# Twenty instead of sixteen tokens of the second tile gathered in the expert layer, 172 instead of 176 dense columns

## What is computed

```python
def one_block(xb):                                   # rows of h, width 2048
    q = (xb @ w_pq).reshape(TOKEN_BLOCK, PEER_HEADS, PEER_DKEY)      # 8 heads, key 256
    s1 = jnp.einsum('thd,kd->thk', q[..., :half], sub_k1)            # 128 keys
    s2 = jnp.einsum('thd,kd->thk', q[..., half:], sub_k2)            # 128 keys
    v1, i1 = lax.top_k(s1, PEER_TOPK)                                # 16
    v2, i2 = lax.top_k(s2, PEER_TOPK)
    best, pos = lax.top_k(cand, PEER_TOPK)                           # of 16 x 16 sums
    eidx = jnp.take_along_axis(cidx, pos, axis=-1)                   # i1 * 128 + i2
    gate = jax.nn.softmax(best.astype(jnp.float32), axis=-1)
    u = expert_u[eidx]                                               # 16384 experts, 2048 wide
    act = jax.nn.gelu(jnp.einsum('td,thkd->thk', xb, u), approximate=False)
    vv = expert_v[eidx]
    return jnp.einsum('thk,thkd->td', gate * act, vv)
```

## Time and profile before

| | |
|---|---|
| median of 3 runs | 2197.24 us |
| the profiled execution | 2204.14 us, span 2202.3 us |
| PE busy | 2130.4 us, 97% |
| DVE busy | 1266.8 us, 58% |
| ACT / POOL busy | 299.2 us / 372.1 us |
| DMA | 853.72 MB, mean 388 GB/s; 838.39 MB read from HBM |
| queues | SP's 47.7%, POOL's 39.5%, ACT's 8.1% of 16 engines' span |

### The profile page before, as it was taken

One profiled execution on the slowest core, in us unless ns is written; L12 is line 12 of the kernel. 1 busy time (PEld: TensorE's weight loads), 2 busy tenths in 40 slices (PEclk: granted clock), 3 DMA queues, 4 the chain that ended last, 5 costly groups with the idle time before them and its releaser, 6 DMA issues.

```text
span 2202.3 us, 36988 instructions
## 1 busy us (share of the span) xinstructions
PE 2130.4 (97%) x14900; PEld 2037.0 (92%) x14900; DVE 1266.8 (58%) x2329; ACT 299.2 (14%) x951; POOL 372.1 (17%) x414
## 2 busy tenths in 40 slices
PE   8999998898899999999999999999999999999997
PEld 6799996686699989999999999999999999999996
DVE  4454447534575378688885467778544444444445
ACT  3000007412310121111111013222000000000002
POOL 0000001123111012222221122222111111111210
PEclk9999999999999999999999999999999999999998
DMA  8999997699698979999999999999999999999996
GB/s 333 405 410 416 394 367 295 243 404 409 245 355 353 366 301 364 387 417 419 422 420 422 420 417 413 413 394 420 420 422 422 422 422 422 421 422 420 420 422 247
DMA packets 126497, 853.72 MB, mean 388 GB/s; under 512 B 14560, under 2 KB 24928, under 8 KB 39488
## 3 DMA queue, kind: packets, MB, share of 16 engines
q1 hardware_dynamic: 58416, 424.43, 47.7%
q0 software_dynamic: 54128, 354.58, 39.5%
q10 hardware_dynamic: 13856, 73.41, 8.1%
HBM read 838.39 MB, written 81.05 MB: 417 GB/s over the span
## 4 chain that ended last, share of the span: by engine, by line
DMA 57%; PE 20%; DVE 13%; issue 5%; ACT 3%; POOL 1%; SPq 0%; DVEq 0%; POOLq 0%; ACTq 0%
DMA BIG<-expert_v,VB 28%; DMA BIG<-expert_u,VB 20%; PE low L1573 11%; PE big L1573 9%; DMA WR<-wall 6%; DVE BIG L1388 4%; DVE XT L1401 3%; DMA BIG<-kaT 2%; DMA BIG<-va 1%; DVE BIG L1328 1%; ACT BIG L710 1%; DVE BIG L1325 1%; DVE BIG L1332 0%; ACT BIG L722 0%; POOL BIG L601 0%
## 5 line engine op out<-in xcount | busy, mean ns | idle before, releaser
L1573 PE MATMUL low<-HT,WR 128*128 128x176 f32 (+3 forms) x6040 | 896.3, 310 | 10.6 <-DVE BIG L1023 7.1
L1573 PEld LDWEIGHTS low<-HT,WR 128*128 128x128 f32 x6040 | 883.7, 191 | 14.0 <-issue 9.3
L1401 DVE SCALAR_TENSOR_TENSOR XT<-BIG,VB,XT 128x2048 f32<-128x2048 f32 x128 | 301.0, 2351 | 341.5 <-DMA BIG<-expert_v,VB 341.4
L1573 PE MATMUL big<-BIG,WR 128*128 (+4 forms) x2952 | 451.0, 308 | 2.5 <-DMA WR<-expert_v 1.8
L1573 PEld LDWEIGHTS big<-BIG,WR 128*128 128x128 f32 x2952 | 430.5, 192 | 4.7 <-issue 3.1
L1388 DVE SCALAR_TENSOR_TENSOR BIG<-BIG 128x2048 f32<-128x2048 f32 x144 | 329.8, 2291 | 179.6 <-DMA BIG<-expert_u,VB 178.1
L1573 PE MATMUL low<-BIG,WR 128*128 (+3 forms) x2552 | 415.8, 318 | 8.4 <-DVE BIG L986 8.4
L1573 PEld LDWEIGHTS low<-BIG,WR 128*128 128x128 f32 x2552 | 395.7, 191 | 10.5 <-issue 8.4
L615 POOL DMA_INDIRECT BIG<-expert_u,VB x144 | 169.3, 1176 | 694.2 <-DVE BIG L1388 620.4
L621 POOL DMA_INDIRECT BIG<-expert_v,VB x144 | 139.6, 970 | 591.0 <-DVE XT L1401 516.1
L1573 PE MATMUL big<-BIG 128*32 128x256 f32 (+6 forms) x1122 | 120.4, 364 | 7.8 <-DMA BIG<-va 2.5
(11 more groups left out here) (258 smaller groups left out, 1295.9 us busy)
## 6 DMA issues: line engine op xcount, KB each, us to landing
WR<-uT SPq DMA_DIRECT2D x128, 1024.0 KB, 9.9
WR<-wall SPq DMA_DIRECT2D x121, 1024.0 KB, 9.3
WR<-expert_v SPq DMA_DIRECT2D x66, 1024.0 KB, 9.4
WR<-expert_v ACTq DMA_DIRECT2D x62, 1024.0 KB, 9.3
BIG<-kaT POOLq DMA_DIRECT2D x64, 384.0 KB, 12.9
BIG<-va POOLq DMA_DIRECT2D x48, 512.0 KB, 13.4
bias_scratch<-BIG ACTq DMA_DIRECT2D x1, 6128.0 KB, 167.3
WR<-bias_scratch SPq DMA_DIRECT2D x4, 1024.0 KB, 16.4
```

What stands on the lines that cost most here:

```text
L1401: nc.vector.scalar_tensor_tensor(out=x_tok, in0=rows_of(row), scalar=weight, in1=x_tok, op0=ALU.mult, op1=ALU.add).then_inc(s_vsum, 1)
L1573: return nc.tensor.matmul(out, lhsT, rhs, start=start, stop=stop, skip_group_check=True)
```

## The change

Four more tokens of the second tile (numbers 144 to 147 of all) leave the dense part and are gathered. 4 tokens x 128 experts are 512 rows, four gathers of `expert_u` and four of `expert_v`. On the partitions stand head, quarter of the choices, and token (`chosen[t:P:MORE, ...]`). `h_more` is a new buffer of 128 x 2048 like `h_few`; for it `BIG` grows, and the reserve of SBUF for GpSimd's DMA descriptors is set to 8192 bytes of each partition (`dynamic_dma_scratch_size`; nothing was given before). `DENSE` goes from 176 to 172, the maps from 44 to 43, `ROWS` from 144 to 148. `DOTS_DONE` comes out as 107 instead of 104, and 22 instead of 25 rows of v fit into the chunks up to 124.

```diff
-FEW = 16
+FEW, MORE = 16, 4
+TAKEN = FEW + MORE
-DENSE = REST - FEW
+DENSE = REST - TAKEN
-MAP_LO, MAP_HI = 80, 124
+MAP_LO, MAP_HI = 80, 123
-ROWS = SLOTS + FEW
+ROWS = SLOTS + TAKEN
...
-        BIG = region("BIG", NCH * DENSE + (URING + 2) * D)
+        AT_FEW = NCH * (REST - FEW)
+        BIG = region("BIG", AT_FEW + (URING + 3) * D)
...
+        h_more = BIG[:, AT_FEW + (URING + 2) * D:AT_FEW + (URING + 3) * D]
...
-                    pool.wait_ge(s_few, 16 * PH)
+                    pool.wait_ge(s_few, 16 * (PH + 2 * MORE))
...
                     keep_rows(3, h_few, big)
+                    keep_rows(4, h_more, big)
...
             for h in range(PH):
-                act.dma_start(chosen[FEW * h:FEW * (h + 1), :, SLOTS:ROWS], few_src[:, :, h * PK:(h + 1) * PK]).then_inc(s_few, 16)
+                act.dma_start(chosen[FEW * h:FEW * (h + 1), :, SLOTS:SLOTS + FEW], few_src[0:FEW, :, h * PK:(h + 1) * PK]).then_inc(s_few, 16)
+            for t in range(MORE):
+                for z in range(2):
+                    act.dma_start(chosen[t:P:MORE, z, SLOTS + FEW:ROWS], few_src[FEW + t:FEW + t + 1, z, :].rearrange("p (r j) -> p r j", j=MORE)).then_inc(s_few, 16)
...
-                nc.vector.scalar_tensor_tensor(out=u, in0=u, scalar=1.0, in1=h_tok if n < SLOTS else h_few, op0=ALU.mult, op1=ALU.mult, accum_out=dots[:, n:n + 1]).then_inc(s_udot, 1)
+                nc.vector.scalar_tensor_tensor(out=u, in0=u, scalar=1.0, in1=h_tok if n < SLOTS else h_few if n < SLOTS + FEW else h_more, op0=ALU.mult, op1=ALU.mult, accum_out=dots[:, n:n + 1]).then_inc(s_udot, 1)
...
+                elif n == FEW:
+                    nc.vector.tensor_scalar(h_more, row, weight, None, ALU.mult).then_inc(s_vsum, 1)
+                elif n < TAKEN:
+                    nc.vector.scalar_tensor_tensor(out=h_more, in0=row, scalar=weight, in1=h_more, op0=ALU.mult, op1=ALU.add).then_inc(s_vsum, 1)
...
+            nc.vector.tensor_copy(h_more.rearrange("p (k r t) -> p k r t", k=KT, t=MORE), HT_by[:, :, P + FEW:P + TAKEN].unsqueeze(2).broadcast_to([P, KT, P // MORE, MORE])).then_inc(s_rep, 1)
...
-            dve.wait_ge(s_few, 16 * PH)
+            dve.wait_ge(s_few, 16 * (PH + 2 * MORE))
...
                     turn_rows(h_few, P)
-            pe.wait_ge(s_ht, 3)
+                    pe.wait_ge(s_rep, 2)
+                    pe.wait_ge(s_ht, 3)
+                    turn_rows(h_more, P)
+            pe.wait_ge(s_ht, 4)
...
-                return mm(u_out[r], WR[:, slot_of(r) * D + k * P:slot_of(r) * D + (k + 1) * P], HT[:, k * NT + P + FEW:(k + 1) * NT], start=(k == 0), stop=(k == KT - 1))
+                return mm(u_out[r], WR[:, slot_of(r) * D + k * P:slot_of(r) * D + (k + 1) * P], HT[:, k * NT + P + TAKEN:(k + 1) * NT], start=(k == 0), stop=(k == KT - 1))
...
-            pe.wait_ge(s_vsum, FEW)
+            pe.wait_ge(s_vsum, TAKEN)
             for k in range(KT):
                 mm(v_all[k][:, 0:FEW], h_few[:, k * P:(k + 1) * P], pick, start=False, stop=True)
+                mm(v_all[k][:, FEW:TAKEN], h_more[:, k * P:(k + 1) * P], pick_more, start=False, stop=True)
...
-    nc = bacc.Bacc("TRN2", target_bir_lowering=False, num_devices=1)
+    nc = bacc.Bacc("TRN2", target_bir_lowering=False, num_devices=1, dynamic_dma_scratch_size=8192)
```

More of the change, by code:

```diff
@@ L292, in build @@
         C_by = C.rearrange("p (c t) -> p c t", t=DENSE)
-        h_few = BIG[:, NCH * DENSE:NCH * DENSE + D]
-        u_ring = [BIG[:, NCH * DENSE + (1 + r) * D:NCH * DENSE + (2 + r) * D] for r in range(URING)]
-        h_tok = BIG[:, NCH * DENSE + (URING + 1) * D:NCH * DENSE + (URING + 2) * D]
+        h_few = BIG[:, AT_FEW:AT_FEW + D]
+        u_ring = [BIG[:, AT_FEW + (1 + r) * D:AT_FEW + (2 + r) * D] for r in range(URING)]
+        h_tok = BIG[:, AT_FEW + (URING + 1) * D:AT_FEW + (URING + 2) * D]
+        h_more = BIG[:, AT_FEW + (URING + 2) * D:AT_FEW + (URING + 3) * D]
         v_ring = u_ring + [h_tok]
@@ L316, in build @@
         gate = [gates[:, 0:SLOTS], hole[15], hole[5][:, 0:64]]
-        few_src = HT[0:FEW, :].rearrange("p (k t) -> p k t", t=NT)[:, 14:16, 0:P]
+        few_src = HT[0:TAKEN, :].rearrange("p (k t) -> p k t", t=NT)[:, 14:16, 0:P]
         pick = VB[:, 3 * ROWS + 3 * DENSE:3 * ROWS + 3 * DENSE + FEW]
+        pick_more = VB[:, 3 * ROWS + 3 * DENSE + FEW:3 * ROWS + 3 * DENSE + TAKEN]
         exp_f = [[tk[:, 2048:2176], tk[:, 2176:2304]], [hole[0], hole[1]], [hole[3][:, 0:64], hole[4][:, 0:64]]]
@@ L432, in v_slot @@
         def v_slot(n):
-            return SLOTS + n if n < FEW else n - FEW
+            return SLOTS + n if n < TAKEN else n - TAKEN
         def chunk_wait(eng, c):
@@ L1421, in _ @@
                         nc.vector.tensor_scalar(own_head[:, h, :], ident, is_head[:, h:h + 1], None, ALU.mult)
+                    nc.vector.tensor_reduce(pick_more, ident.rearrange("p (r t) -> p t r", t=MORE), AX_X, ALU.add)
                     link(nc.vector.tensor_reduce(pick, ident.rearrange("p (h t) -> p t h", t=FEW), AX_X, ALU.add))
@@ L1477, in _ @@
                     if not later:
-                        first = slice(0, FEW)
+                        first = slice(0, TAKEN)
                         link(nc.vector.scalar_tensor_tensor(out=eidx_f[first], in0=exp_f[1][0][first], scalar=float(NKEY), in1=exp_f[1][1][first], op0=ALU.mult, op1=ALU.add))
@@ L1487, in _ @@
             dve.wait_ge(s_turn, 1)
-            dve.wait_ge(s_few, 16 * PH)
-            own = P - FEW
+            dve.wait_ge(s_few, 16 * (PH + 2 * MORE))
+            own = P - TAKEN
             for z in range(3):
-                nc.vector.tensor_copy(turned[z][:, 0:own], bank[6][:, z * P + FEW:(z + 1) * P])
+                nc.vector.tensor_copy(turned[z][:, 0:own], bank[6][:, z * P + TAKEN:(z + 1) * P])
                 nc.vector.tensor_copy(turned[z][0:64, own:DENSE], bank[7][0:64, z * 64:(z + 1) * 64])
@@ L2085, in dense_v @@
                         pe.wait_ge(s_dev, NCH - UB + k // 2 + 1)
-                    ins = mm(v_all[k][:, FEW:REST], WR[:, slot_of(r) * D + k * P:slot_of(r) * D + (k + 1) * P], coefs, start=(first and k % 2 == 0), stop=False)
+                    ins = mm(v_all[k][:, TAKEN:REST], WR[:, slot_of(r) * D + k * P:slot_of(r) * D + (k + 1) * P], coefs, start=(first and k % 2 == 0), stop=False)
                 ins.then_inc(s_used, 1)
```

4 lines of the change are left out of this document (2 added, 2 removed).

## The result

| | before | changed |
|---|---|---|
| median, same chip | 2197.05 us (4 runs, 2193.14 to 2197.28) | 2225.20 us (4 runs, 2217.97 to 2225.74) |
| ratio | | 1.012, 95% interval 1.0098 to 1.0142 |
| the profiled execution | 2204.14 us, span 2202.3 | 2217.97 us, span 2216.0 |

A forecast was written before the change was run, and what follows sets the result against it. DMA engines and PE are full together, and the gathers end last: +19.9 us for eight gathers, -3 in the gate stage, +1 in 818 to 935 us, about +18; on 2197.24 that gives 2215.2 us, range 2206 to 2223.

The forecast's parts named there:

- rival A: Full stretches: DMA engines have room up to 435 GB/s, PE ends last, faster at 2173 us; chance 0.06.
- B: Half room: gate stage and run-out fill wholly, late phase at 424 GB/s or more; within 4 us of before; chance 0.04.
- C: Smaller descriptor reserve throttles POOL to two gathers in flight, 7.7 us per gather, +500 us; chance 0.02.
- D: Dense matmuls: 172 columns run no faster than 176, PE ends about 2190, same time as forecast; no chance given.
- +19.9 us for 8.39 MB: DMA engines: eight more gathers of 128 rows x 8192 bytes cost 19.9 us at 421 GB/s.
- "I take back 3 us": Gate maps, 1297 to 1550 us: room between 410 and 421 GB/s, 6.6 us at most, hides 3 us of the gathers.
- "+1 us": 818 to 935 us: PE comes 4.2 us later, moving up to 2.2 us of stream into the full stretch; 1 us added.
- The picks: 16 extra PE matmuls with `pick_more`, 32 records of 4 columns: 3.7 us more on PE.
- The base: The median of the kernel before, 2197.24 us, to which the +18 us was added.
- PE: -20.3 forecast: PE's sum: -27.3 us for narrower columns, -0.9 one map fewer, +4.2 transposes of `h_more`, +3.7 matmuls with `pick_more`.
- The wait at the maps: First gate map: PE expected to wait about 6 us for the gathers' rows, and some more in the maps.
- What would show it: Signs listed for the changed kernel's profile: record spacing, gather pace and rate, PE's wait and lead, end spacing, tail.

The follow-up runs named there:

- Half chunks: Changed kernel with 16 of the dense v chunks loaded only half, 8.39 MB fewer in the stream: 2202.49 us, ratio to before 1.0029.
- twice the gathers: Changed kernel with the step made twice: eight more tokens gathered than before, 168 dense columns, 42 gate maps: 2249.19 us, ratio to before 1.0236.
- the reserve alone: Kernel before with only the reserve for GpSimd's DMA descriptors set to 8192 bytes per partition: 2198.61 us, ratio to before 0.9995.
- the gathers alone: Changed kernel but with 176 dense columns and 44 maps as before, four tokens counted twice: 2224.1 us, ratio to before 1.0096.

## Why the prediction missed by 10 us

- **What bounds the kernel: right.** Stream and gathers share full engines, and the gathers end last. Half chunks speed the gathers up by just their bytes, and PE's columns, given back or taken away, move nothing.
- **The rate doesn't rise: right.** 420 GB/s in the full stretches of the changed kernel, 419 and 420 with twice the gathers. No stretch of 100 us or more that I read in any run stood above 422, and rival A falls with it. B falls too, C by the reserve alone, D by the spacing of the records. The Trainium skill, DMA: Bandwidth & Descriptors, Specifications, has the ceiling at 435 GB/s; the rates here stay 3% under it.
- **+19.9 us for 8.39 MB: right** as far as bytes go. 8.39 MB less in the stream gave 19.8 us in the medians and 18.5 in the stretch.
- **"I take back 3 us" in the gate stage: the step that failed.** I took the gap between 410 and 421 GB/s for room that more gathers would fill. On the mean the unfilled time there went from 7.1 us to 8.0, where I had it fall to 4: 4 us wrong. The single profiles scatter by more than the difference (5.5 to 10.5; the change's own two are 10.5 and 8.1), so a growth isn't shown, but none came down to 4, and with the drain removed four more gathers filled nothing either (4.1 and 4.7 us on the mean). In the drain no gather is asked for: POOL stands for 11 to 12 us. Why the rest can't be used isn't shown; that DVE's rows and PE's maps follow each other chunk by chunk through a ring of three is my reading of the program.
- **"+1 us" in the first 100 us: too small**, it was 1.9, and all of it lies in the first 20 us, at the second transposes. **Nothing for the stages between**, where 0.9 and 2.0 us came: the 2.0 at the picks, the 0.9 mostly in one of the three profiles. These four differences, 4 + 1 + 1 + 2, are the 7.5 us between the forecast of 18 and the 25.5 of the stretch.
- **The picks: wrong on PE.** 3.7 us more were forecast; 4.8 and 6.6 came in the two profiles of the change, and 2 more in the chunk behind. By count the price was right: the first 32 records of the stop took 3.5 us at the upper clock level, and so would the other 32. What came on top is the lower clock, which no row of the trace before had shown there.
- **The base.** The medians put the change 28.2 and 27.3 us over before, the gathers alone 23.8; the stretch has 25.5. The forecast was put on three runs within 0.4 us of each other, of a kernel whose runs reach from 2189.4 to 2207.4. The range ended at +26 us, with nothing in it for that scatter; 2 us more would have held the result.
- **PE: -20.3 forecast, 0.7 later in fact** on the count from the transposes (1353.9 for 1353.2). That 2173.5 still lies in my 2163 to 2175 is luck: the stages ahead took 10.9 us less. In the first profile the 21 us are, to half a microsecond, these: the weight loads stood 7.6 us in the u chunks instead of 0.8 (6.8 more); the waits at the maps were 5.9 instead of 2.2 us and those for v chunks 4.1 instead of 1.8 (6.0 more); and at the lower clock PE lost some 8.5 us, none before. Of these 8.5 a good 3 are at the picks, the others behind waits of 1.9 us and more: at 1578.7 us PE waited 2.3 us for a chunk, and its next 16 records took 4.05 us instead of 2.33, so this wait cost PE 1.7 us more than its length.
- **The wait at the maps: right in size, by luck.** I had put 6 us at the first gate map, since row 113 and the first map had waited before. In neither profile of the change did PE wait at the first map. The 5.9 us (5.7 in the second profile) stand where u passes to v. The larger of the two waits in the first profile, 3.9 us, came right after DVE had waited 4.05 and 5.48 us for the first v gathers, so that the map behind them was late.
- **What would show it:** records 145.9 ns apart (forecast 145.7); PE 20 us ahead of the last v row (15 or more); 420 GB/s in the v chunks; gathers alone 2.5 us apart; tail 22.7 us. These came as forecast, the wait at the first map did not. The gathers' pace in the v chunks was 5.21 us over the whole 500 us, not 5.3 or more; but up to 2000 us, ahead of the picks, PE did 2745 records for 2684 and POOL started 75 gathers for 77, one per 5.33 us (76 and 5.26 in the second profile). So the faster stream did push the gathers back; in the next 100 us, with the stop at the picks in them, POOL started 21.

## What to carry to other kernels

Where two resources are full together, find which one ends last, and price a move between them by what it adds to that one; 20 us taken off an engine that is 97% busy were worth nothing here, and 8.4 MB on the full DMA engines cost their full time and a quarter more. A stage that runs some per cent under the full rate is no proof of room: here none of it could be had for four more gathers. Look first for drains, in which nothing is asked for, and price every new stop of the engine that frees the buffers also by the bytes that don't flow meanwhile (2 us at the transposes here). And before a range is closed, see how wide the runs of the old kernel scatter; three runs within 0.4 us came from a kernel whose runs span 18.
